# Halving the exponentials of the global attention heads, one half for each score bank

## The reference, cut to what matters

```python
def global_gqa(q, k, v):          # q: 8 heads, k and v: 2 heads, 64 channels each
    ...
    def one(qblk):                # a block of 128 queries
        s = jnp.einsum('bqkgd,bskd->bkgqs', qblk, k).astype(jnp.float32) * scale
        p = jax.nn.softmax(s, axis=-1).astype(v.dtype)
        return jnp.einsum('bkgqs,bskd->bqkgd', p, v)
    ...

for l in range(DEPTH):            # DEPTH = 2; l = 0 is the even layer
    h = rmsnorm(x, norm_gain[l])
    ...
    ya = global_gqa(qa, ka, va)       # "global heads", the change is here
    yb = window_gqa(qb, kb, vb, sink_b[e], rel_bias)
    ym = memory_attn(qm, mk, mv)
    y = jnp.concatenate([ya, yb, ym], axis=-1) * jax.nn.silu(gate)
    x = x + y @ w_out_even[e]
```

## Time and profile before

| | |
|---|---|
| Median of 3 runs | 2379.98 us (2376.65 to 2381.43) |
| The profiled execution's own time | 2380.79 us |
| Its span, first to last instruction | 2379.0 us |
| Busy: PE, PEld, DVE, ACT, POOL | 96%, 81%, 67%, 55%, 32% |
| Mean granted TensorE clock | 0.990 of full |
| Global scores | 249.4 to 563 us from the span's start |

### The profile page before, as it was taken

One profiled execution on the slowest core, in us unless ns is written; L12 is line 12 of the kernel. 1 busy time (PEld: TensorE's weight loads), 2 busy tenths in 40 slices (PEclk: granted clock), 3 DMA queues, 4 the chain that ended last, 5 costly groups with the idle time before them and its releaser, 6 DMA issues.

```text
span 2379.0 us, 35445 instructions
## 1 busy us (share of the span) xinstructions
PE 2279.6 (96%) x11782; PEld 1936.5 (81%) x11782; DVE 1601.5 (67%) x3239; ACT 1313.6 (55%) x3030; POOL 750.1 (32%) x909
## 2 busy tenths in 40 slices
PE   6999999999999999999999999898998999999999
PEld 6888788888888878888888888787777888887887
DVE  7443677677886333346665566668789788889787
ACT  6444566666775434456656566555555545455532
POOL 5555232311235642222222222558774300000000
PEclk9999999999999999999999999999999999999999
DMA  7322111111233342322332233532343633345734
GB/s 225 113 76 66 38 27 32 32 34 43 61 119 109 100 131 67 94 67 88 90 94 76 87 93 91 185 90 78 92 160 98 200 106 111 112 141 177 229 111 139
DMA packets 333316, 242.73 MB, mean 102 GB/s; under 512 B 66384, under 2 KB 286800, under 8 KB 332624
## 3 DMA queue, kind: packets, MB, share of 16 engines
q1 hardware_dynamic: 333136, 240.47, 33.3%
HBM read 196.64 MB, written 43.78 MB: 101 GB/s over the span
## 4 chain that ended last, share of the span: by engine, by line
PE 74%; DVE 11%; issue 5%; ACT 4%; POOL 4%; DMA 1%; SPq 0%; DVEq 0%; POOLq 0%; ACTq 0%
PE PS L1922 13%; PE PS L1924 13%; PE PS L1923 13%; PE PS L2161 6%; PE PS L2162 6%; PE PS L2163 6%; PE PS L2068 5%; PE PS L2035 5%; PE PS L2022 2%; PE PS L2023 2%; POOL WS L2822 2%; ACT PY L2172 1%; PE PS L2077 1%; DMA WR<-in_ffn_in 1%; DVE ST L2530 1%
## 5 line engine op out<-in xcount | busy, mean ns | idle before, releaser
L2822 POOL TENSOR_TENSOR WS<-WR,WS 128x256 fp32r<-128x256 f32 x638 | 493.9, 793 | 981.6 <-ACT WS L2172 980.5
L1922 PE MATMUL PS<-HT,WS 128*128 128x512 f32 x1488 | 602.7, 405 | 26.8 <-DVE X L2464 5.4
L1924 PE MATMUL PS<-HT,WS 128*128 128x512 f32 x1488 | 584.5, 393 | 0.0
L1923 PE MATMUL PS<-HT,WS 128*128 128x512 f32 x1488 | 582.6, 392 | 0.0
L1922 PEld LDWEIGHTS PS<-HT,WS 128*128 128x128 f32 x1488 | 281.6, 189 | 86.6 <-issue 17.7
L1924 PEld LDWEIGHTS PS<-HT,WS 128*128 128x128 f32 x1488 | 281.0, 189 | 61.5
L1923 PEld LDWEIGHTS PS<-HT,WS 128*128 128x128 f32 x1488 | 282.0, 190 | 51.9
L2172 ACT ACTIVATE PT<-PS 128x512 fp32r<-128x512 f32 x352 | 186.1, 529 | 211.4 <-PE PS L2035 211.1
L2172 ACT ACTIVATE WS<-WR 128x256 fp32r<-128x256 f32 x662 | 247.3, 410 | 93.0 <-PE PS L1924 54.2
L2420 DVE TENSOR_TENSOR PT<-PS,PT 128x512 fp32r<-128x512 f32 x352 | 211.6, 609 | 93.3 <-ACT PT L2172 90.9
L2068 PE MATMUL PS<-PT,QKV 128*128 128x256 f32 (+1 forms) x1248 | 208.8, 289 | 3.2 <-DVE YB L2599 2.3
(11 more groups left out here) (288 smaller groups left out, 4653.0 us busy)
## 6 DMA issues: line engine op xcount, KB each, us to landing
WR<-in_w_in_odd SPq DMA_DIRECT2D x106, 256.0 KB, 2.9
EO<-in_grid SPq DMA_DIRECT2D x48, 384.0 KB, 3.1
WR<-in_ffn_in SPq DMA_DIRECT2D x64, 256.0 KB, 3.0
WR<-in_w_in_even SPq DMA_DIRECT2D x100, 128.0 KB, 2.6
WR<-in_w_out_odd SPq DMA_DIRECT2D x48, 256.0 KB, 2.8
yd<-PY SPq DMA_DIRECT2D x44, 256.0 KB, 3.3
EO<-in_ffn_in SPq DMA_DIRECT2D x35, 256.0 KB, 3.0
WR<-in_w_in_even SPq DMA_DIRECT2D x34, 256.0 KB, 3.0
```

Source lines behind the costliest of these rows:

```text
L1922: e.matmul(out, wh, rh, start=start, stop=False)
L1923: e.matmul(out, wh, rl, start=False, stop=False)
L1924: return e.matmul(out, wl, rh, start=False, stop=stop)
L2822: e.tensor_tensor(ws(i, 1, n), RAW[raw_slot(u)][:, o:o + n], f32(ws(i, 0, n)), ALU.subtract).then_inc(s_wlop.sem, 1)
```

## The change

For a wide score the exponential becomes two activations of 512 columns. The first reads the first bank and raises a new semaphore `s_exp1`; the second reads the second bank and raises `s_exp` as before. Each leaves its own row sum: in `st[:, 2:3]` and `st[:, 3:4]`. TensorE's wait for the first bank is now on `s_exp1`, that for the second on `s_exp`. VectorE adds the two sums before the reciprocal, with a wait of its own for the addition's result. The window and memory chunks and the odd layer are left as they are.

```diff
+        s_exp1 = signal("s_exp1")
...
         def exps(s):
             s_exp.add()
+            if s.c.wide:
+                s.exp1 = s_exp1.add()
...
         def recip(s):
-            s_rec.add(1 if s.c.sink is None else 2)
+            s_rec.add(1 if s.c.sink is None and not s.c.wide else 2)
...
-                        until[b] = (s_exp, s.no) if c.bias is None else (s_mx, s.mx)
+                        until[b] = (s_mx, s.mx) if c.bias else (s_exp1, s.exp1) if c.wide and i == 0 else (s_exp, s.no)
...
-                        act(two_parts(p, s.cut), src, ACT.Exp, bias=st[:, 1:2], accum_out=st[:, 2:3]).then_inc(s_exp.sem, 1)
+                        if s.c.wide:
+                            act(p[:, 0:512], src[:, 0, :], ACT.Exp, bias=st[:, 1:2], accum_out=st[:, 2:3]).then_inc(s_exp1.sem, 1)
+                            act(p[:, 512:1024], src[:, 1, :], ACT.Exp, bias=st[:, 1:2], accum_out=st[:, 3:4]).then_inc(s_exp.sem, 1)
+                        else:
+                            act(two_parts(p, s.cut), src, ACT.Exp, bias=st[:, 1:2], accum_out=st[:, 2:3]).then_inc(s_exp.sem, 1)
...
                         w.wait_ge(s_rec, s.rec - 1)
+                    elif s.c.wide:
+                        w.wait_ge(s_exp1, s.exp1)
+                        e.tensor_tensor(den, den, st[:, 3:4], ALU.add).then_inc(s_rec.sem, 1)
+                        w.wait_ge(s_rec, s.rec - 1)
                     w.wait_ge(s_spread, s.spread)
```

## The result

The changed kernel takes 2398.24 us (median of 6 runs, 2397.49 to 2401.39), beside 2379.91 us for the kernel before in runs on the same chip: the ratio is 1.0075, 95% interval 1.0064 to 1.0087. It is 18 us slower, and outside the range of the forecast, 2369 to 2385 us. The profiled execution has a span of 2399.6 us, that of the kernel before 2379.0.

The account below looks back on a forecast made before the run. TensorE, busy 96%, was taken as the bound. From the profiled 2380.79 us, - 6.0 (stalled scores) + 2.0 (given back) + 0.4 (addition) = 2377.2 us, a median of 2376.4; forecast 2376.5 us, range 2369 to 2385 us.

Parts of the forecast that it names:

- What bounds the kernel: TensorE, busy 96%; in the 64 global scores' stretch, 24 stalled scores lose 18.9 us waiting for score banks, a ceiling.
- The halves' durations: Each 512-column exponential steps by 0.68 us; the first bank comes free at 0.84 us, the second at 1.52 us.
- What a stalled score gains, and what the longer exponentials cost: 24 stalled scores gain 0.25 us each, 6.0 us; longer exponentials on ScalarE give back 2.0 us in 8 stalls.
- the second rival: The gain turns into a later wait, TensorE stalling longer at the next score: 2380 us, chance 0.16.
- The addition: Two additions add 0.36 us to each of 32 jobs on VectorE, mostly hidden: 0.4 us charged, bounds 0 and 11.5.
- The cover of the values: Values' matmuls have 0.9 us of cover behind VectorE's low part; 0.4 us remains, so the delay there costs nothing.
- The clock: Two 3.4 us drops to 1.2 GHz in the stretch cost 1.7 us each; possible removal counted only in the range.
- the rival: The first rival: gain kept everywhere and both clock drops avoided, 10.8 us less, 2369.2 us; chance 0.22.
- The third: Rival: exponential, copy, low part, reciprocals and maximum bound a job, costing 0.86 us each; slower, 2388 us, chance 0.17.
- My three signs of being wrong: Exponential step over 0.8 us; values' matmuls waiting for the low part; stretch 4 us shorter but the rest longer.

Follow-up runs that it names:

- no_add: The change without the addition of the two row sums (the reciprocal reads another column, so outputs are not scaled by the softmax's sum): 2382.45 us, ratio 1.0002.
- scalar_add: The change with the addition written as a tensor_scalar, its second operand a per-partition scalar: 2393.2 us, ratio 1.0043.
- moved: The change with each global job's additions and reciprocals moved on VectorE to behind the job's last turned bank: 2399.74 us, ratio 1.0071.

## Why the prediction was wrong

**What bounds the kernel.** Right in part. 17.5 us of the loss arise in the stretch, and most of it in TensorE's waits for its banks. But the idle time before the first matmuls, which I took as the sign, rose only from 14.4 to 17.1 us (the prediction had it fall). The rest stands before the second bank's matmuls, where I expected a small idle time and the profile shows none, and before transposes that wait for VectorE, which I had not looked at.

**The halves' durations.** Right to 0.02 us. The step is 0.68 us as forecast; the first bank starts at 0.83 us (forecast 0.84), the second at 1.50 us (1.52).

**What a stalled score gains, and what the longer exponentials cost.** Too favourable. The forecast of the two terms was a gain of 6.0 us against 2.0 given back, -4.0 us or -0.17%. Without the addition the balance is 0, interval -0.11% to +0.15%: just outside. The traces of before and `no_add`, one execution each, show where it went. Ahead of the first matmuls the starts came 6.1 us closer together in all; ahead of the second bank's two matmuls they grew by the same 6.1 us. The 24 scores that had stalled keep 2.0 us, where 4.0 were forecast. I had let the pause between the banks cost one restart of 0.10 us, but it lengthens both of the steps that follow, by 4.7 us in the 24. The 40 others "have nothing to gain", but they have something to lose, since their second bank too comes free 0.26 us later: eight of them now pause before it, and the 40 lose 1.3 us, where I charged nothing. So the number 0 is that of the second rival, to which I gave 0.16, but the mechanism is a pause within the score, not longer stalls at the next one: the scores with a loss of 0.2 us or more before their first matmul fell from 24 to 13.

**The addition.** This is the step that failed, and it gave the sign of the result. I charged 0.4 us, with 11.5 as the upper bound; the runs say 0.73% (1.0075 - 1.0002), about 17 us. It failed twice. First the duration: 0.18 us was read off a pair of a window chunk at 709.86, while four additions of the same line lasted 0.24 to 0.57 us near 592 and 602 us of the trace before, and those four too end 15 to 17 ns after an instruction of GpSimd. In the change 30 of 64 are held, most of them since ScalarE's weight split follows the copy behind the exponential and starts GpSimd just as VectorE comes to the addition. The additions last 22.9 us in all, and a job's section grew by 0.82 us (1.03 - 0.21), not by 0.36. Second the cover: "elsewhere VectorE waits afterwards, for a copy or a score, and hides it". It does wait afterwards, but the maximum comes first. It was already over 0.1 us late in 38 of 64 scores of the trace before (the prediction counted 33), and is in 58 in the change. With the split the copy and the low part ahead of the section are also later. So `scalar_add`, held nowhere, still loses 0.41% against `no_add`, 10 us, which is nearly my upper bound, while the same instructions ahead of the low part lose nothing.

**The cover of the values.** Right. The low parts are not what TensorE waits for. In the kernel after, its values' matmuls waited 0.2 us for one in all.

**The clock.** It went the other way than the rival had it, for little. The window view of the kernel after has three intervals' worth at 1.2 GHz in place of the two of before:

```profile
278.77:282.18 3.41, 3.41 (x19) 3.41 (x18) 2.64 (x5) 1.94 (x6) 1.18 (x2) 0.50 0.25 56
493.81:500.64 6.83, 5.80 (x18) 4.86 (x18) 1.95 (x4) 1.45 (x4) 0.73 (x1) 0.50 0.17 38
```

At half speed the 3.4 us more cost at most 1.7 of the 17.5 us. In the stretch of `no_add`'s trace there is no such interval, which makes up to 3.4 us for it; without that its stretch of 310.4 us would be no shorter than the 312.3 of before.

**The rivals.** The third was right in sign and in mechanism: maxima that come late by copy, low part and sum. I priced it at 0.86 us a job and 2388 us. With held additions the section's own extra is not 0.36 but (22.9 + 64 x 0.03)/32 = 0.78 us a job, with 0.03 us from each addition's end to its reciprocal (446.16 to 446.19). Together with 0.5 us of longer exponentials that is 1.3 us a job, up to 41 us in 32 jobs; net 17.5 were measured. I gave this rival 0.17, on the ground that VectorE is idle for 93 us of the stretch. That is an average, and says nothing about the place ahead of the maximum. My three signs of being wrong stayed silent, too, but for 0.2 us of one value matmul: they look at ScalarE's step, the values' matmuls and the rest of the kernel, none at VectorE ahead of the maximum.

## What to carry to other kernels

A split that frees a resource earlier has to be priced with everything that it repeats: here what the first bank gained, the pause before the second took back, also in scores that had not stalled. A tiny instruction added on VectorE costs what its place costs: ask what stands behind it in the queue, and whether two SBUF operands put it against GpSimd's work there. The same instructions moved into a gap of VectorE cost nothing. And a pause of TensorE inside a group of matmuls can be missing from the idle times: compare the distances of starts.

## What the hardware showed that I had not expected

- An addition of 128x1 lasts 0.16 us, or up to 1.25 us when GpSimd is at work; every long one in the change and in `moved` ends within 20 ns of a GpSimd instruction. As tensor_scalar with the second operand a per-partition scalar in SBUF it lasts 0.19 to 0.22 us in all 256 cases of four kernels, and is never held.
- After a pause between two matmuls of 512 columns not only the one behind the pause is late, the next starts 0.34 us after it and not 0.23 us (450.74 and 451.08 above).
- A reduction of 128x4 to 128x2 and a reciprocal of 128x2 last 150 and 167 ns (means of 32), as little as on one column, so that two scores' sums take no longer than one's:

```profile
L2582 DVE RECIPROCAL RD<-ST 128x2 f32<-128x2 f32 x32 | 5.3, 167 | 1.1
L2578 DVE TENSOR_REDUCE ST<-ST 128x2 f32<-128x4 f32 x32 | 4.8, 150 | 0.0
```
